# A hybrid decoder trunk on one core: the groups that end in the residual stream are added to h by VectorE straight from PSUM

## The reference

```python
h = x
for i in range(2):
    hn = rms_norm(h, norm_mix_g[i])
    mix = conv_recurrent_mixer(hn, ...) if i % 2 == 0 else stick_breaking_mixer(hn, ...)
    h = h + mix                                    # output projection, 2048 x 2048
    h = h + square(relu(rms_norm(h, g) @ w_up[i])) @ w_down[i]     # 2048 -> 8192 -> 2048
    gate = sigmoid(rms_norm(h, g) @ w_ple_gate[i])
    h = h + (p[i] @ w_ple_proj[i]) * gate
return rms_norm(h, norm_f_g)
```

## Time and profile before

| | |
|---|---|
| device time, median of 3 runs | 2388.08 us (2386.59 to 2389.94) |
| the profiled execution | 2388.35 us, its span 2386.6 us |
| instructions in the trace | 39036 |
| mean granted clock of TensorE, as a share of 2.4 GHz | 0.995 |

### The profile page before, as it was taken

One profiled execution on the slowest core, in us unless ns is written; L12 is line 12 of the kernel. 1 busy time (PEld: TensorE's weight loads), 2 busy tenths in 40 slices (PEclk: granted clock), 3 DMA queues, 4 the chain that ended last, 5 costly groups with the idle time before them and its releaser, 6 DMA issues.

```text
span 2386.6 us, 39036 instructions
## 1 busy us (share of the span) xinstructions
PE 2336.7 (98%) x13578; PEld 2048.7 (86%) x13578; DVE 1575.7 (66%) x1894; ACT 1276.1 (53%) x1606; POOL 22.7 (1%) x31
## 2 busy tenths in 40 slices
PE   7999999999999999999999999999999999999997
PEld 6888988888888888888888888888888888888886
DVE  6889986656655555667776666766556556556665
ACT  5676575444444445555565666555445445445553
POOL 0001100000000000000000000000000000000000
PEclk9999999999999999999999999999999999999998
DMA  6659856556556555555655545656565565555543
GB/s 216 204 149 216 221 167 192 190 187 189 189 187 191 186 189 188 185 191 169 194 176 172 169 153 174 195 184 195 186 192 186 188 190 186 191 186 184 193 160 105
DMA packets 440595, 439.46 MB, mean 184 GB/s; under 512 B 13392, under 2 KB 438480, under 8 KB 440528
## 3 DMA queue, kind: packets, MB, share of 16 engines
q1 hardware_dynamic: 432080, 430.20, 56.8%
q0 software_dynamic: 8448, 8.39, 2.6%
HBM read 428.05 MB, written 2.10 MB: 180 GB/s over the span
## 4 chain that ended last, share of the span: by engine, by line
PE 85%; DVE 6%; DMA 4%; ACT 2%; issue 2%; DVEq 0%; SPq 0%; ACTq 0%
PE ps L439 53%; PE ps L445 26%; PE ps L437 2%; DVE spl L1107 2%; DMA spl<-raw 2%; DMA raw<-in_w_out 1%; PE ps L443 1%; ACT spl L705 1%; DVE y L1447 0%; DMA raw<-in_w_in 0%; DVE tv L1143 0%; PE O L568 0%; PE Z L542 0%; DMA raw<-in_w_o 0%; PE Z L551 0%
## 5 line engine op out<-in xcount | busy, mean ns | idle before, releaser
L1107 DVE TENSOR_TENSOR spl<-raw,spl 128x1024 fp32r<-128x1024 f32 x794 | 959.7, 1223 | 535.1 <-ACT spl L705 504.7
L705 ACT ACTIVATE spl<-raw 128x1024 fp32r<-128x1024 f32 x826 | 857.6, 1054 | 673.4 <-PE ps L445 589.0
L439 PE MATMUL ps<-XA,spl 128*128 128x512 f32 x3072 | 973.3, 398 | 26.0 <-DVE spl L1107 17.6
L439 PE MATMUL ps<-XB,spl 128*128 128x512 f32 x2944 | 926.0, 396 | 2.7 <-ACT pp L705 2.7
L445 PEld LDWEIGHTS ps<-XA,spl 128*128 128x128 f32 x3072 | 580.4, 189 | 137.6
L445 PEld LDWEIGHTS ps<-XB,spl 128*128 128x128 f32 x2944 | 553.0, 188 | 130.7
L445 PE MATMUL ps<-XA,spl 128*128 128x256 f32 x3072 | 606.3, 279 | 0.0
L445 PE MATMUL ps<-XB,spl 128*128 128x256 f32 x2944 | 578.4, 278 | 0.0
L439 PEld LDWEIGHTS ps<-XA,spl 128*128 128x128 f32 x3072 | 471.5, 190 | 28.5 <-issue 11.5
L439 PEld LDWEIGHTS ps<-XB,spl 128*128 128x128 f32 x2944 | 448.2, 189 | 3.3 <-issue 2.9
L1143 DVE TENSOR_TENSOR tv<-cross,ps 128x512 f32<-128x512 f32 x199 | 135.7, 682 | 39.8 <-ACT cross L705 39.5
(11 more groups left out here) (161 smaller groups left out, 1084.9 us busy)
## 6 DMA issues: line engine op xcount, KB each, us to landing
raw<-in_w_up SPq DMA_DIRECT2D x256, 512.0 KB, 3.7
raw<-in_w_down SPq DMA_DIRECT2D x256, 512.0 KB, 3.8
raw<-in_w_qkv SPq DMA_DIRECT2D x96, 512.0 KB, 4.4
raw<-in_w_in SPq DMA_DIRECT2D x64, 512.0 KB, 4.7
raw<-in_w_gate SPq DMA_DIRECT2D x64, 512.0 KB, 4.3
raw<-in_w_out SPq DMA_DIRECT2D x32, 512.0 KB, 4.8
raw<-in_w_o SPq DMA_DIRECT2D x32, 512.0 KB, 4.5
spl<-raw POOLq DMA_DIRECT2D x16, 512.0 KB, 6.4
```

Source lines behind the costliest of these rows:

```text
L439: pe.matmul(ps[:, b + o, :], w[:, q, 0, c], x[:, kt, :, :], start=start, stop=False)
L705: return act.activation(out, in_, ACT.Copy, scale=scale)
L1107: dve.tensor_tensor(s[:, :, 1, :], raw[:, m % NRAW, :, :], s[:, :, 0, :].bitcast(F32), ALU.subtract).then_inc(lo_ready, 1)
```

## The change

80 groups end in h with nothing between: 8 of OUTA, 8 of OUT1, 64 down groups. For them ScalarE makes no cross copy. VectorE waits for the group's last chunk itself (`add_ps`), adds the cross halves to h, waits for that operation (`res_cross`), adds the other halves to h, and counts `sum_ready` with the second. `add_h` stays for the gate groups alone. ScalarE's `residual` waits for `sum_ready` of that group instead of `res_ready`. `crossed` counts the copies that are left. In OUTA the order on VectorE becomes: split, two adds, split, `residual`; on ScalarE the copy ahead of the two splits goes.

```diff
@@ scalar
-            def group(g, gi, m, it, first=False, later=0, steps={}):
+            def group(g, gi, m, it, first=False, later=0, steps={}, direct=False):
                 if not first:
                     period(m, it, 4 - later)
-                    take_cross(g, gi, group_done(m, it))
+                    if not direct:
+                        take_cross(g, gi, group_done(m, it))
...
-            def residual(hidx, t0, n, X):
-                act.wait_ge(res_ready, hidx + 1)
+            def residual(added, hidx, t0, n, X):
+                act.wait_ge(*added)
...
                 for s in range(4):
                     m = C_OUTA + 2 * s
-                    take_cross(G_OUTA + s, i * 4, (chunk_used, i * 8 + (m + 2)))
                     period(m, i, 2)
-                    residual(i * 4 + (H_OUTA + s), i * 8 + 2 * s, 1, XA)
+                    residual((sum_ready, i * 4 + (G_OUTA + s + 1)), i * 4 + (H_OUTA + s), i * 8 + 2 * s, 1, XA)
@@ vector
+            def add_ps(g, gi, done, hidx, t0):
+                b = 2 * (g % 2)
+                ht = h[:, bass.ds(t0, 2), :]
+                dve.wait_ge(chunk_used, done)
+                if counts(g - 7, gi):
+                    dve.wait_ge(sum_ready, gi + (g - 7))
+                dve.tensor_tensor(ht, ht, ps[:, b:b + 2, 256:512], ALU.add).then_inc(res_cross, 1)
+                dve.wait_ge(res_cross, hidx - (8 if g >= G_OUT1 else 0) + 1)
+                dve.tensor_tensor(ht, ht, ps[:, b:b + 2, 0:256], ALU.add).then_inc(sum_ready, 1)
...
-                take_sum(g, gi)
+                if direct is None:
+                    take_sum(g, gi, ci=ci)
+                else:
+                    done = m + 3 + s if first else it * 8 + (m + 4)
+                    add_ps(g, gi, done, *direct)
...
             def down(g, gi, m, it, hidx, t0, first=False, later=0, steps={}):
-                group(g, gi, m, it, first, later, steps)
+                group(g, gi, m, it, first, later, steps, direct=(hidx, t0))
                 dve.wait_ge(sum_ready, gi + (g + 1))
-                add_h(hidx, t0)
...
                 for s in range(4):
-                    take_sum(G_OUTA + s, i * 4)
                     split(C_OUTA + 2 * s + NSPL, i)
+                    add_ps(G_OUTA + s, i * 4, i * 8 + (C_OUTA + 2 * s + 2), i * 4 + (H_OUTA + s), i * 8 + 2 * s)
+                    split(C_OUTA + 2 * s + 1 + NSPL, i)
                     dve.wait_ge(sum_ready, i * 4 + (G_OUTA + s + 1))
-                    add_h(i * 4 + (H_OUTA + s), i * 8 + 2 * s, first=True)
-                    split(C_OUTA + 2 * s + 1 + NSPL, i)
                     residual(i * 4 + (8 + s), i * 8 + 2 * s, 1, XA)
```

More of the change, by code:

```diff
@@ L189, in trunk @@
         res_ready = sem("res_ready")
+        res_cross = sem("res_cross")
         sq_ready = sem("sq_ready")
@@ L261, in crossed @@
         def crossed(g):
-            return g - (16 if g >= G_OUTA else 0) - (8 if g >= G_OUT1 else 0)
+            for base, end, n in ((G_MLP0, G_GATE0, 16), (G_MLP1, G_GATE1, 80)):
+                if base <= g < end:
+                    return n + (g - base) // 16 * 8 + (g - base) % 16
+            for base, n in ((G_GATE1, 112), (G_QKV, 56), (G_GATE0, 48)):
+                if g >= base:
+                    return n + g - base
+            return g
         def lo_there(engine, m, it):
@@ L748, in group @@
                         split(m + NSPL + q)
-                    take_cross(g, 0, (chunk_used, m + 7 + s))
+                    if not direct:
+                        take_cross(g, 0, (chunk_used, m + 7 + s))
             def norm(n, columns=False):
@@ L800, in gate @@
                     split(m + 3 + NSPL, it)
-                residual(hidx, t0, n, X)
+                residual((res_ready, k + 1), hidx, t0, n, X)
             def out_groups(g, m, hidx, n, X, first=None):
@@ L806, in out_groups @@
                     for s in range(2):
-                        group(g + s, 0, m + 4 * s, 0, True, steps=first)
-                        residual(hidx + s, 2 * s, n, X)
+                        group(g + s, 0, m + 4 * s, 0, True, steps=first, direct=True)
+                        residual((sum_ready, g + s + 1), hidx + s, 2 * s, n, X)
                 with act.Fori(1 if first else 0, 4) as i:
                     for s in range(2):
-                        group(g + s, i * 2, m + 4 * s, i, later=1)
+                        group(g + s, i * 2, m + 4 * s, i, later=1, direct=True)
                         split(m + 4 * s + 3 + NSPL, i)
-                        residual(i * 2 + (hidx + s), i * 4 + 2 * s, n, X)
+                        residual((sum_ready, i * 2 + (g + s + 1)), i * 2 + (hidx + s), i * 4 + 2 * s, n, X)
             def mlp(g, m, u, hidx, norm_in, hid, n, X):
@@ L822, in mlp @@
                     for s in range(2):
-                        group(g + 8 + s, i * 2, m + 32 + 4 * s, i)
+                        group(g + 8 + s, i * 2, m + 32 + 4 * s, i, direct=True)
                 with act.Fori(1, 3) as f:
@@ L830, in mlp @@
                         for s in range(2):
-                            group(g + 8 + s, f * 16 + i * 2, m + 32 + 4 * s, f * 8 + i)
+                            group(g + 8 + s, f * 16 + i * 2, m + 32 + 4 * s, f * 8 + i, direct=True)
                 g, m, u, hidx = g + 48, m + 192, u + 24, hidx + 24
@@ L1119, in period, with group @@
                     split(m + NSPL + q, it)
-            def group(g, gi, m, it, first=False, later=0, steps={}):
+            def group(g, gi, m, it, first=False, later=0, steps={}, ci=None, direct=None):
                 if not first:
@@ L1137, in lo_of, with take_sum @@
                                          ALU.subtract)
-            def take_sum(g, gi, out=None):
+            def add_ps(g, gi, done, hidx, t0):
                 b = 2 * (g % 2)
-                dve.wait_ge(cross_copied, gi + (crossed(g) + 1))
+                ht = h[:, bass.ds(t0, 2), :]
[5 more added lines that the diff above has]
+                dve.tensor_tensor(ht, ht, ps[:, b:b + 2, 0:256], ALU.add).then_inc(sum_ready, 1)
+            def take_sum(g, gi, out=None, ci=None):
+                b = 2 * (g % 2)
+                dve.wait_ge(cross_copied, (gi if ci is None else ci) + (crossed(g) + 1))
                 dve.tensor_tensor(tv[:, :, :] if out is None else out, cross[:, :, :], ps[:, b:b + 2, 0:256],
@@ L1180, in res_los, with add_h @@
                 r.then_inc(res_tiles, 1)
-            def add_h(hidx, t0, first=False):
-                if not first:
-                    dve.wait_ge(res_ready, hidx - 7)
+            def add_h(k, t0):
                 ht = h[:, bass.ds(t0, 2), :]
                 dve.tensor_tensor(ht, ht, tv[:, :, :], ALU.add).then_inc(res_ready, 1)
-                dve.wait_ge(res_ready, hidx + 1)
+                dve.wait_ge(res_ready, k + 1)
             def residual(f, t0, n, X):
@@ L1193, in residual, with up @@
                     res_los(f, t0, n, X)
-            def up(g, gi, m, it, u, t0, hid, norm_n=None, first=False):
-                group(g, gi, m, it, first)
+            def up(g, gi, m, it, u, t0, hid, norm_n=None, first=False, ci=None):
+                group(g, gi, m, it, first, ci=ci)
                 if norm_n is not None:
@@ L1221, in gate @@
                 dve.wait_ge(gate_mul, k + 1)
-                add_h(hidx, t0)
+                add_h(k, t0)
                 if not first:
@@ L1252, in mlp @@
                             up(g + s, f * 16 + i * 2, m + 4 * s, f * 8 + i, f * 8 + i * 2 + (u + s),
[L1253 removed]
+                               i * 4 + 2 * s, hid, ci=f * 8 + i * 2)
                     with dve.Fori(0, 4) as i:
```

## The result

| | before | changed |
|---|---|---|
| median of 20 runs each, us | 2389.91 (2386.59 to 2394.15) | 2394.19 (2390.71 to 2397.78) |
| ratio, 95% interval | | 1.0016 (1.0010 to 1.0022) |
| profiled execution, its span, us | 2388.35, 2386.6 | 2395.57, 2393.8 |

The change makes the kernel slower by 0.16%, 3.8 us; 0.18% was forecast. The two medians lie 4.3 us apart. The changed kernel was measured twice more, each time beside the kernel before: 1.0005 (0.9996 to 1.0015) and 1.0016 (1.0006 to 1.0026). The single executions of one kernel scatter by 3 to 4 us to either side, about as much as the effect, so what follows rests on stage times of traces and takes the ratios only as a check.

A forecast was written before the change was run, and what follows sets the result against it. The prediction took TensorE, busy for 98% of the span, as the bound. It summed 2388.35 + 3.45 (OUTA) + 0.92 (OUT1) = 2392.7, less 0.27: 2392.4 us, with a range of 2389.0 to 2395.8.

The forecast's parts named there:

- The places: OUTA and the start of OUT1 lose time, +3.45 and +0.92 us; the 64 MLP groups cost 0.
- OUTA's term: OUTA, 8 groups: VectorE's cycle of 5.75 us sets the pace, MLP0's second chunk waits until 361.5; +3.45 us.
- the signs that I had named for being wrong: OUTA's cycle under 5.57 us, a wait in an MLP, or the low clock lasting longer than three steps.
- The 0.28 us that it read as a dependence: VectorE's idle time in OUTA's 5.63 us cycle before the change, taken as a dependence inside.
- the chained adds cost no gap: Rival, chance 0.06: second add starts 0.60 us after the first; +0.85 us in OUTA, +0.60 in OUT1, total 2389.5.
- OUT1's term: Start of OUT1: group 144's second add ends later than the old sum; +0.92 us, a wait of 1.3 us.
- The new wait of 1.6 us at the third group: OUTA: TensorE wants the bank pair at 319.64, but the second add ends at 321.20.
- The clock: Behind OUTA's last wait: granted clock falls as before, 1.75 us, net 0; none assumed after waits of 1.6 and 1.3 us.
- The total: Whole kernel: 2392.4 us, 0.18% above the time before; forecast's chance 0.56.
- the copy was the limit: Rival, chance 0.04: without the copy VectorE catches up in OUTA, both waits go; 4.15 us less, 2383.9.

The follow-up runs named there:

- the shift with copies: The kernel before, copies kept, with OUTA's sum ahead of the split of chunk 94 and all splits one place back; ratio to before 0.9993 (0.9984 to 1.0002).

## Why the prediction was right, and where not

**The places.** Both were right: OUTA and OUT1 carry the cost, the MLPs none. The sum counted from the rounding of chunk 95 on, and in the changed order this is what starts the chain.

**OUTA's term was too large**: +3.45 us forecast, 1.81 measured from the same anchor. The mechanism held, and the step that failed is a size: "The two adds depend on each other, so they start 0.92 us apart". They start 0.71 us apart. The 0.92 us of rows 8 held register work of VectorE's queue, three values for the place in h and two waits between sum and add; in the changed kernel the first add has computed h's place already, and one value is left. Those 0.2 us, in the first pair and in seven cycles, make the 1.6 us by which the term was too large. The 0.72 us at OUT1's first sum, the very group of the second term, could have been read from the trace of before. The cycle became 5.55 instead of 5.75 us. A cycle under 5.57 was among the signs that I had named for being wrong, and it came: VectorE is not the slower engine in the changed cycle, as the prediction had it, but only starts late. The 0.28 us that it read as a dependence are in part of the same kind: they are gone in OUT1's first groups and in the loop written out. With the register work put back, the stretch from the rounding of chunk 95 is 43.91 us; the sum had 361.5 - 317.37 = 44.13. So the working holds with the price that it took, and the price was wrong for this pair. The rival *the chained adds cost no gap* put the term at 0.85 us, with 0.60 us between the adds; the truth lies between. The Trainium skill's sentence that a semaphore between chained operations costs nothing extra (VectorE: DVE Perf Modes, the section on the DRAIN) comes out nearer than I said: where the second waits for the first they start 0.71 us apart, where it doesn't 0.60 (358.40 to 359.00), so 0.11 us and not 0.24 are the wait's.

**OUT1's term**: +0.92 forecast, +0.72 measured, by the same step. In one of three executions the wait was 1.57 us; ScalarE had waited 1.60 us for the load of the last chunk rounded ahead of the adds there, and for no load at that chunk in the first.

**The new wait of 1.6 us at the third group** did not appear in the changed kernel's three traces. The granted clock fell at OUTA's first matmuls in each, so TensorE itself came later (the steps took 1.28 us); VectorE's pace swallowed that, as the prediction had said of a fall after the new wait. In two edited kernels there was a wait, of 0.97 and 0.67 us, where the load had landed a microsecond later.

**The clock** was taken as it fell behind OUTA in the trace of before, price 1.75 us. Windows behind the wait, in the changed kernel and in the one with the adds ahead of the split (length, busy and count by engine, PEclk):

```profile
367.00:369.00 2.00, 2.00 (x8) 1.67 (x8) 1.85 (x3) 0.15 (x1) 0.00 (x0) 0.57 0.83 250
```

```profile
360.00:362.00 2.00, 2.00 (x13) 1.78 (x12) 2.00 (x3) 2.00 (x4) 0.00 (x0) 1.00 0.06 16
```

Behind waits of 2.05 and 2.03 us one fell and the other did not. At this place it fell after 1.90, 1.96, 2.03, 2.05 and 2.20 us and stayed after 1.21, 1.33, 2.03, 2.25 and 2.64. At OUTA's first matmuls, after 2.73 to 2.75 us, it fell in 8 traces of 12. The length of the wait alone doesn't decide. A fall behind OUTA costs 1.55 us, less than the 1.75 of the prediction: from MLP0's second chunk to the next wait, that wait left out, are 867.58 to 867.60 us in the five traces with a fall, and 866.02 to 866.05 in the five with a wait of over 1 us there and no fall. The forecast left the fall out on both sides, and it did come in all three traces of the changed kernel as in the one of before. That it had to, no run shows.

**The total** agrees with the forecast better than its terms do, and that is luck: 2.5 us stand in the traces, 4.4 were summed, and the first comparison has 3.8 (2.4 to 5.3). The 2.5 us lie inside all three intervals of the changed kernel. What more there may be is open. If the clock falls more often in the changed kernel, each fall behind OUTA costs 1.55 us, but three executions with a profile can't show how often. OUTA's first matmul comes 1.2 to 5.0 us later in those three than in the one trace of before, but 2.1 later also in the shift with copies, whose code is the kernel before's up to the last split ahead of OUTA.

**The rival "the copy was the limit"** fell as the rows had said: no wait of TensorE shrank in the edited stages when the copy went.

## What to carry to other kernels

Moving work off an engine that isn't the bound bought nothing here by itself, and the order that came with the move had a price. Ask at which point of the slower engine's cycle the buffer is given back, and put that point first. Where the two cycles lie close (5.55 to 5.63 us against 5.57 here), look for what starts the stage's chain, here a load, and check in each trace that the engine did wait for it. Counted from there, five executions with the same order agree to 0.03 us, where whole executions scatter by microseconds. Before taking a distance between two instructions from another place of the program, look whether that place is in a loop and what its queue computes between them. The direct adds leave tv free, so they can be moved ahead of the previous group's residual; the kernel that does so was faster, but it also has OUTA's loop written out, and which of the two did it is not shown.

## What the runs showed of the hardware

- Two dependent VectorE operations of 128x512 start 0.71 to 0.72 us apart, with one register value of a loop computed between them (357.68, 358.40) or with none (1495.91, 1496.63 before). They start 0.90 to 0.92 apart with three (356.90, 357.80; rows 8), and 0.60 where the second doesn't wait for the first. So more waits on counts long reached cost nothing visible with constants, and 0.2 us with two more values from registers.
- Two executions of the same changed kernel, the first and the third: the clock fell after a wait of 3.27 us in one and stayed in the other (the columns are start and duration; two matmuls take 1.22 against 0.73 us, and the granted clock of the next 2 us is 0.50 against 1.00).

```profile
72.81 1.22 PE L447 MATMUL ps<-XA,spl 128*128 128x512 f32 x2 [3.27 <-DVE tv L1167]
```

```profile
72.65 0.73 PE L447 MATMUL ps<-XA,spl 128*128 128x512 f32 x2 [3.27 <-DVE tv L1167]
```
